# Expert weights in 16 KB pieces per partition, and the order of features that goes with it

## What is computed

```python
mod = c_act @ ada_w[layer] + ada_b[layer]
sh_a, sc_a, g_a, sh_f, sc_f, g_f = jnp.split(mod, 6, axis=-1)
...
h = modulate(rmsnorm(x, norm_ffn[layer]), sh_f, sc_f)
...
g_logits = (h @ w_group) + b_group            # 4 groups
e_logits = (h @ w_expert) + b_expert          # 32 experts
...
(jax.nn.silu(xb @ w_gate[e]) * (xb @ w_up[e])) @ w_down[e]   # 1024 -> 512 -> 1024
...
return jnp.zeros_like(h).at[row_tok].add(ys * row_w[:, None])
```

## Time and profile before

| | before |
|---|---|
| median of 3 runs | 1907.51 us (1904.16 to 1908.43) |
| profiled execution, span | 1901.0 us |
| TensorE busy | 1736.3 us, 91% |
| VectorE busy | 547.8 us, 29% |
| ScalarE busy | 414.4 us, 22% |
| GpSimd busy | 115.6 us, 6% |
| moved by DMA | 548.26 MB in 186871 packets |
| of it on q1 | 492.85 MB in 153536 packets |
| gathers and scatters | 40 and 38 |

### The profile page before, as it was taken

How to read it: one execution, slowest core, us unless ns; L and a number is a source line. 1 busy time by engine, 2 the same in 40 slices (tenths; PEclk the granted TensorE clock), 3 DMA queues, 4 the chain that set the end, 5 groups by cost and what they waited for, 6 DMA issues and landing times.

```text
span 1901.0 us, 17119 instructions
## 1 busy us (share of the span) xinstructions
PE 1736.3 (91%) x6504; PEld 780.1 (41%) x6504; DVE 547.8 (29%) x1218; ACT 414.4 (22%) x1024; POOL 115.6 (6%) x123
## 2 busy tenths in 40 slices
PE   5999998999988889989798999998899988998897
PEld 2455555443433333333344455543433333333332
DVE  2675564431111011101576122225501111111113
ACT  3133354311111011111310234342211111111110
POOL 1000001010000000000000000002000000000000
PEclk9999998999999999999899999999999999999999
DMA  9972423389999999999766021021599999999996
GB/s 347 370 273 84 182 89 136 133 324 380 410 409 410 409 408 406 391 398 395 272 221 221 0 86 48 26 108 59 228 408 410 410 410 408 407 405 405 398 397 256
DMA packets 186871, 548.26 MB, mean 288 GB/s; under 512 B 12345, under 2 KB 49706, under 8 KB 185758
## 3 DMA queue, kind: packets, MB, share of 16 engines
q1 hardware_dynamic: 153536, 492.85, 66.8%
q0 software_dynamic: 15840, 36.64, 5.2%
q10 hardware_dynamic: 17406, 17.59, 2.9%
HBM read 536.66 MB, written 34.63 MB: 301 GB/s over the span
## 4 chain that ended last, share of the span: by engine, by line
PE 65%; DMA 21%; SPq 6%; DVE 5%; issue 2%; ACT 1%; ACTq 0%; DVEq 0%
PE psum L2137 19%; DMA ring<-in_moe_w_up_dram 14%; PE psum L1890 9%; PE psum L1688 9%; PE psum L2170 7%; SPq L447 6%; DMA XN<-in_moe_w_up_dram 4%; PE psum L1743 3%; PE psum L1860 3%; DVE W L1078 1%; DMA XN<-in_moe_w_gate_dram 1%; PE psum L2115 1%; PE psum L1717 1%; PE psum L1617 1%; PE psum L1995 1%
## 5 line engine op out<-in xcount | busy, mean ns | idle before, releaser
L2137 PE MATMUL psum<-ring,V 128*64 128x512 f32 (+1 forms) x1648 | 500.8, 628 | 75.7 <-DMA ring<-in_moe_w_up_dram 49.5
L2137 PEld LDWEIGHTS psum<-ring,V 128*64 128x64 f32 (+1 forms) x1648 | 175.0, 154 | 351.6 <-issue 345.2
L2170 PE MATMUL psum<-ring,V 128*64 128x512 f32 (+1 forms) x832 | 225.1, 597 | 8.2 <-issue 5.1
L973 ACT ACTIVATE V<-psum,modall,scls 128x128 f32<-128x128 f32 x312 | 117.2, 456 | 494.0 <-PE psum L2115 494.0
L1078 DVE SCALAR_TENSOR_TENSOR W<-ring,cact,W 128x512 f32<-128x512 f32 (+1 forms) x224 | 138.5, 618 | 7.7
L1487 DVE TENSOR_TENSOR V<-V,psum 128x512 f32<-128x512 f32 x40 | 27.5, 688 | 378.1 <-PE psum L2137 378.1
L2137 PE MATMUL psum<-XN,V 128*64 128x512 f32 (+1 forms) x288 | 130.7, 607 | 5.4 <-DMA ring<-in_moe_w_up_dram 3.2
L1503 DVE SCALAR_TENSOR_TENSOR HT<-psum,slot_gate,W 128x512 f32<-128x512 f32 x80 | 60.1, 751 | 256.3 <-PE psum L2170 256.3
L2170 PEld LDWEIGHTS psum<-ring,V 128*64 128x64 f32 (+1 forms) x832 | 72.3, 144 | 109.5 <-issue 109.5
L1688 PE MATMUL psum<-HT,ring 128*128 128x512 f32 x256 | 115.4, 597 | 0.0
L982 ACT ACTIVATE V<-psum 128x512 f32<-128x512 f32 x40 | 23.9, 597 | 377.4 <-PE psum L2137 377.4
(11 more groups left out here) (307 smaller groups left out, 1734.2 us busy)
## 6 DMA issues: line engine op xcount, KB each, us to landing
ring<-in_moe_w_gate_dram SPq DMA_DIRECT2D x52, 2048.0 KB, 24.1
ring<-in_moe_w_down_dram SPq DMA_DIRECT2D x52, 2048.0 KB, 24.9
ring<-in_moe_w_up_dram SPq DMA_DIRECT2D x51, 2048.0 KB, 24.9
ring<-in_ada_w_dram SPq DMA_DIRECT2D x16, 2048.0 KB, 15.6
XN<-in_moe_w_gate_dram SPq DMA_DIRECT2D x9, 2048.0 KB, 24.8
XN<-in_moe_w_up_dram SPq DMA_DIRECT2D x9, 2048.0 KB, 26.0
ring<-in_ada_w_dram ACTq DMA_DIRECT2D x16, 1024.0 KB, 5.3
XN<-in_moe_w_down_dram SPq DMA_DIRECT2D x7, 2048.0 KB, 25.8
```

The costliest lines, as they stand in the source:

```text
L973: ins = act.activation(V[:, 2 * D + b * D + k * P:2 * D + b * D + (k + 1) * P], bank[0][:, q * P:(q + 1) * P], ACT.Identity, bias=mod[:, 2 ...
L2137: ins = pe.matmul(bank[2 + 2 * i + b][half * w:(half + 1) * w, :], V[:, col:col + w], slot3(x)[:, k, :], start=(k == 0), stop=(k == KC - 1))
L2170: ins = pe.matmul(bank[6 + hf][half * w:(half + 1) * w, :], V[:, col:col + w], slot3(x, 4)[:, k, hf * HALF:(hf + 1) * HALF], start=(k == 0 ...
```

## The change

The order of features becomes one in which a partition's rows are neighbours in DRAM. For gate and up step k takes feature 8 p + k for partition p, for down it takes 4 p + k. A load is then one contiguous piece of 16 KB for each partition, 128 pieces instead of 512, into the same place. The second norm writes in the new order, reading X with a step of 8 elements; the router weights and the bias columns are loaded in it, by 2 loads instead of 4 and in pieces of 32 bytes instead of 8. A block of 512 modulation features fills only 64 of the 128 partitions in the new order, in 8 columns, so its sum becomes 8 products of 64 columns instead of 4 of 128; a half becomes 8 products of 32 columns instead of 2 of 128. For down, silu and the gate product read PSUM with a step of 4 elements and write V in order. The path for overfull experts, which does not run here, is changed likewise.

```diff
@@ -380,6 +380,14 @@
 
         half_in = [sem(f"half_in{i}") for i in range(2)]
 
+        def ffn_block(i):
+
+            return slice(64 * (i % 2), 64 * (i % 2) + 64), 24 + KC * ((i - 6) // 2), KC * ((i - 6) // 2)
+
+        def ffn_half(i):
+
+            return slice(32 * (i % 4), 32 * (i % 4) + 32), 88 + KC * ((i - 4) // 4), KC * (3 + (i - 4) // 4)
+
         def half_slot(i):
             return ring[:, 5, 2048 * (i % 2):2048 * (i % 2 + 1)].rearrange("p (k n) -> p k n", k=KC)
 
...
@@ -390,14 +398,17 @@
 
             eng.wait_ge(w_in[SLOT[n]], ARRIVED[n])
 
-        def by_pairs(a):
-            return a.rearrange("(a p j) -> p a j", p=P, j=2)
-
         def expert_weights(l, e):
-            g = t["moe_w_gate"][l, ds(e, 1)].rearrange("o (a p j) n -> p (o a) (j n)", p=P, j=2)
-            u = t["moe_w_up"][l, ds(e, 1)].rearrange("o (a p j) n -> p (o a) (j n)", p=P, j=2)
-            d = t["moe_w_down"][l, ds(e, 1)].rearrange("o (k p) n -> p (o k) n", p=P)
+            g = t["moe_w_gate"][l, ds(e, 1)].rearrange("o (p j) n -> p (o j n)", j=KC)
+            u = t["moe_w_up"][l, ds(e, 1)].rearrange("o (p j) n -> p (o j n)", j=KC)
+            d = t["moe_w_down"][l, ds(e, 1)].rearrange("o (p j) n -> p (o j n)", j=4)
             return g, u, d
+
+        def by_fours(a):
+            return a.rearrange("p (q j) -> p j q", j=4)
+
+        def four(a):
+            return a.rearrange("p (j q) -> p j q", j=4)
 
         turned = [sm[1]["pt"], sm[1]["probs"]]
 
...
@@ -517,11 +528,10 @@
                     elif l == 1 and i == 6:
                         sp.wait_ge(*sm[1]["y_added"](2 * TC))
                         sp.wait_ge(*sm[1]["gate_pe"](2))
+                    slot_free(m + i)
+                    sp.dma_start(slot(m + i), {"g": g, "u": u, "d": d}[kind]).then_inc(w_in[SLOT[m + i]], 16)
                     if kind == "d":
-                        load(m + i, d, k=4)
                         del expert[r]
-                    else:
-                        load(m + i, g if kind == "g" else u, k=4)
 
                 rows_back(l)
                 most = sp.value_load(flag[0:1, 0:1], min_val=0, max_val=S)
...
@@ -561,7 +571,7 @@
             for l in range(LAYERS):
                 for i, src in enumerate((t["ada_b"][l, 3 * D:4 * D], t["ada_b"][l, 4 * D:5 * D], t["norm_ffn"][l])):
                     at = (3 * l + i) * KC
-                    pool.dma_start(colF[:, at:at + KC].rearrange("p (a j) -> p a j", j=2), by_pairs(src)).then_inc(col_in, 16)
+                    pool.dma_start(colF[:, at:at + KC], src.rearrange("(p j) -> p j", j=KC)).then_inc(col_in, 16)
             pool.wait_ge(setup_dve, 6)
             pool.dma_start(fb_d, W[0:H, 0:FALL]).then_inc(fb_out, 16)
             pool.wait_ge(fb_out, 16)
...
@@ -592,10 +602,8 @@
                     pool.wait_ge(*s["logits"](N_STEPS))
                 gate_diag(ga_diag[l], mods[l][:, 16:24])
 
-                for j in range(2):
-                    pool.dma_start(rw3[:, j::2, 0:NG], t["moe_w_group"][l].rearrange("(a p j) n -> j p a n", p=P, j=2)[j]).then_inc(s["rw_in"].sem, 16)
-                for j in range(2):
-                    pool.dma_start(rw3[:, j::2, NG:NR], t["moe_w_expert"][l].rearrange("(a p j) n -> j p a n", p=P, j=2)[j]).then_inc(s["rw_in"].sem, 16)
+                pool.dma_start(rw3[:, :, 0:NG], t["moe_w_group"][l].rearrange("(p j) n -> p j n", j=KC)).then_inc(s["rw_in"].sem, 16)
+                pool.dma_start(rw3[:, :, NG:NR], t["moe_w_expert"][l].rearrange("(p j) n -> p j n", j=KC)).then_inc(s["rw_in"].sem, 16)
                 pool.dma_start(rbias[:, 0:NG], t["moe_b_group"][l:l + 1, :].broadcast_to([P, NG])).then_inc(s["rw_in"].sem, 16)
                 pool.dma_start(rbias[:, NG:NR], t["moe_b_expert"][l:l + 1, :].broadcast_to([P, E])).then_inc(s["rw_in"].sem, 16)
 
...
@@ -979,7 +987,7 @@
                     act.wait_ge(*s["gu_pe"](e * 2 + 1))
                     if e >= 2:
                         act.wait_ge(*s["hid_pe"](e - 1))
-                    act.activation(V[:, 4 * D + b * HALF:4 * D + (b + 1) * HALF], bank[2 + b][:, :],
+                    act.activation(four(V[:, 4 * D + b * HALF:4 * D + (b + 1) * HALF]), by_fours(bank[2 + b]),
                                    ACT.Silu).then_inc(s["silu"].sem, 1)
 
                 rows_t(0, 0)
...
@@ -1049,21 +1057,21 @@
-                def normalised(root, ready, c, pairs=False):
+                def normalised(root, ready, c, eights=False):
                     dve.wait_ge(*root(c + 1))
                     step(dve.reciprocal(small[:, 12 + c:13 + c], small[:, 8 + c:9 + c]))
                     to, x = xn3[:, c, :], x3[:, c, :]
-                    if pairs:
-                        to, x = to.rearrange("p (a j q) -> p a j q", j=2, q=P), x.rearrange("p (a q j) -> p a j q", j=2, q=P)
+                    if eights:
+                        to, x = to.rearrange("p (j q) -> p j q", j=KC), x.rearrange("p (q j) -> p j q", j=KC)
                     dve.tensor_scalar(to, x, small[:, 12 + c:13 + c], None, ALU.mult).then_inc(ready.sem, 1)
...
@@ -1082,17 +1090,25 @@
                         ins.then_inc(signal, 1)
 
                 def half_columns(u):
-                    i, n = HALVES_AT[u][0], 2 * len(HALVES_AT[u])
-                    at = 4 * N_MOD0 + 2 * i
                     dve.wait_ge(half_red, u + 1)
-                    bias = colF[:, 3 * KC + 2 * (i - 4):3 * KC + 2 * (i - 4) + n] if 4 <= i < 12 else colA[:, at - 16:at - 16 + n]
-                    dve.tensor_tensor(modall[:, at:at + n], bank[6][:, at:at + n], bias, ALU.add).then_inc(half_col, 1)
+                    for i in HALVES_AT[u]:
+                        at = 4 * N_MOD0 + 2 * i
+                        if 4 <= i < 12:
+                            rows, at, of = ffn_half(i)
+                            ins = dve.tensor_tensor(modall[rows, at:at + KC], bank[6][rows, at:at + KC], colF[rows, of:of + KC], ALU.add)
+                        else:
+                            ins = dve.tensor_tensor(modall[:, at:at + 2], bank[6][:, at:at + 2], colA[:, at - 16:at - 14], ALU.add)
+                    ins.then_inc(half_col, 1)
 
                 def mod_columns(i):
                     dve.wait_ge(mod_red, i + 1)
                     if i == 6:
                         dve.wait_ge(col_in, 16 * 3 * LAYERS)
-                    bias = (colF[:, 4 * (i - 6):4 * (i - 5)] if 6 <= i < 10 else colA[:, 4 * i:4 * i + 4] if i < 12 else
+                    if 6 <= i < 10:
+                        rows, at, of = ffn_block(i)
+                        dve.tensor_tensor(modall[rows, at:at + KC], bank[6][rows, at:at + KC], colF[rows, of:of + KC], ALU.add).then_inc(mod_col, 1)
+                        return
+                    bias = (colA[:, 4 * i:4 * i + 4] if i < 12 else
                             colV[:, V_KAB + 4 * (i - 12):V_KAB + 4 * (i - 11)] if i < 16 else
                             colA[:, 48 + 4 * (i - 16):48 + 4 * (i - 15)])
                     dve.tensor_tensor(modall[:, 4 * i:4 * i + 4], bank[6][:, 4 * i:4 * i + 4], bias, ALU.add).then_inc(mod_col, 1)
...
@@ -1310,7 +1326,7 @@
                     dve.wait_ge(*s["y_added"](u + 1))
                     for ch in norms_at.get(u, ()):
                         mean_square(s["ss2"], s["arg2"], ch)
-                        normalised(s["root2"], s["xn2"], ch, pairs=True)
+                        normalised(s["root2"], s["xn2"], ch, eights=True)
 
                 for k in (2, 3, 6, 7):
                     dve.wait_ge(*s["xt2_pe"](KC // 2 + k // 2 + 1))
...
@@ -1483,8 +1499,8 @@
                 def hidden(e, b):
                     dve.wait_ge(*s["silu"](e + 1))
                     dve.wait_ge(*s["gu_pe"](e * 2 + 2))
-                    at = V[:, 4 * D + b * HALF:4 * D + (b + 1) * HALF]
-                    dve.tensor_tensor(at, at, bank[4 + b][:, :], ALU.mult).then_inc(s["hid"].sem, 1)
+                    at = four(V[:, 4 * D + b * HALF:4 * D + (b + 1) * HALF])
+                    dve.tensor_tensor(at, at, by_fours(bank[4 + b]), ALU.mult).then_inc(s["hid"].sem, 1)
 
                 def hidden_t(e, b):
                     dve.wait_ge(*s["hid_pe"](e + 1))
...
@@ -1612,10 +1628,14 @@
                 else:
                     pe.wait_ge(mod_sum, i - 3)
                 pe.wait_ge(mod_col, i)
-                for j in range(4):
-                    by_two = slice(2 * P * (j // 2) + j % 2, 2 * P * (j // 2 + 1), 2)
-                    ins = pe.matmul(bank[6][:, 4 * i + j:4 * i + j + 1], acc[:, by_two if 6 <= i < 10 else slice(j * P, (j + 1) * P)],
-                                    C[:, C_32:C_32 + 1] if i < 4 else ones[:, 0:1], start=True, stop=True)
+                if 6 <= i < 10:
+                    rows, at, _ = ffn_block(i)
+                    for j in range(KC):
+                        ins = pe.matmul(bank[6][rows, at + j:at + j + 1], acc[:, j::KC], ones[:, 0:1], start=True, stop=True)
+                else:
+                    for j in range(4):
```

(42 more changed lines are left out.)

## The result

The changed kernel takes 1997.94 us (median of 4 runs, 1989.37 to 2008.28) beside 1907.97 us for the kernel before on the same chip (1904.16 to 1908.65): a ratio of 1.049, 95% interval 1.047 to 1.052. It is slower by 90 us, where the forecast said slower by 22 us. The direction was right, the size was not, and the time lies outside the range.

A forecast was written before the change was run, and what follows sets the result against it. Weight transfers were taken to bound the expert stages, with longer pieces making gathers late. Stages +17.5 us and small parts +5 gave 22.5 on 1901.0, 1923.5; with 6.5 to the runs' median, 1930 us, range 1868 to 1955.

The forecast's parts named there:

- Rate: Expert weight loads: 16 KB pieces move at 429 GB/s instead of 410, worth 22 us a layer, 44 in all.
- Turns by packet: DMA engines alternate between weight and row queues packet by packet; a turn grows from 0.27 to 0.69 us, scatter-gather pair 12.4 us.
- The loop: Expert stage: down, scatter, gather, transposes, down form a cycle of 26.5 us a pass, taken as 26.2.
- 7.9 for transposes and down products: Last part of the expert pass cycle: TensorE's transposes of gathered rows and down products, put at 7.9 us.
- worse turns: Rival: two weight packets pass per row packet, turn 1.30 us, expert pass 37.5 us, total over 2300 us; chance 0.13.
- The small parts: Side costs outside the weight loads: modulation columns, halves, norm, PSUM reads and initial column loads, together +5 us (-2 to +16).
- (1): Layer 0 modulation columns, four blocks: eight 64-wide products replace four 128-wide, +0.4 us each, +1.6 on TensorE's path.
- Term (2): Layer 1, eight modulation halves: eight 32-wide products replace two, 0.63 to about 1.0 us each, +2.4 us (0 to 7.2).
- Term (3): Second norm reading X with a step of 8: +0.7 us each (0 to 1.5), +1.4 us in the sum.
- Term (4): Silu and gate product reading PSUM with step 4: open only in each layer's last pass, taken as +0.2 us.
- The gather stays hidden: Rival: expert-stage gathers still hide, leaving only the rate gain, 1868.5 us, or half hidden 1885 to 1903; chance 0.22.
- Pieces cut again: Rival: 16 KB weight pieces are cut into 4 KB packets, leaving only the small parts, 1912.5 us; chance 0.15.

The follow-up runs named there:

- early gathers: Each gather issued one pass sooner, ahead of the scatter it stood behind: on the changed kernel 1884.69 us (ratio 0.990), on the kernel before 1903.3 us (0.999).
- the version by fours: Changed kernel with early gathers, features 512 a + 4 p + j, gate and up in 8 KB pieces, four modulation products: 1883.65 us; with gathers not moved 1887.55 us.

## Why the prediction was right, and where it failed

- *Rate.* Right in kind: 426 GB/s at 16 KB and 420 at 8 KB where 429 and 423 came from the line. Its worth was put at 22 us a layer; where nothing covers it, with early gathers on both sides, the stages fall by 518.9 - 505.2 = 13.7 and 519.3 - 502.3 = 17.0. Most of the rest is in the first pass of each layer, which takes 4.5 and 3.8 us longer, counted from its gather's issue; over the 19 passes behind it the gain is 18.2 (470.6 against 452.4) and 20.8 (469.8 against 449.0). These 452.4 us are 23.8 a pass, so the pace of the weights was put 1 us too high, at 24.8.
- *Turns by packet.* Right. While a scatter and a gather go out beside weights, the two queues of the changed kernel (514 to 524 us: packets, MB, share) take turns one for one, whatever the size of either's packets:

```profile
q1 hardware_dynamic: 264, 3.80, 88.8%
q0 software_dynamic: 263, 0.48, 12.5%
```

  That is 10 x 16 / 264 = 0.61 us a turn in the mean, against 0.69 forecast. The 3.80 MB are 232 pieces of 16 KB; the other 32 of the 264 are small packets, which come with each load, 16 to one (the version with 4 KB pieces, which makes two loads of each of the 192, has 192 x 16 = 3072 packets more on q1 than the kernel before: 156608). In a stretch without rows, 528 to 538 us, they stand alone under 512 B:

```profile
DMA packets 293, 4.28 MB, mean 428 GB/s; under 512 B 32, under 2 KB 32, under 8 KB 32
```

  A full piece took 0.888 x 160 / 232 = 0.61 us and a row 0.125 x 160 / 263 = 0.08. So a turn with a full piece is the forecast's 0.69; what the forecast lacked is that every eighth turn goes against a small packet. The pair of scatter and gather takes 18 x 0.61 = 10.9 us by that, not 12.4. The landings fit. Behind a scatter a gather lands in 8.0, 10.2 and 15.1 us at 4, 8 and 16 KB, 0.59 us for each KB (16 turns of 37 ns); without a scatter ahead of it (early gathers) in 7.4, 8.4 and 10.7, 0.28 for each KB (7 to 8 turns).
- *The loop.* Right, 26.2 us forecast. Measured 28.0 in layer 0 and 27.7 in layer 1 with slow down products; the four passes of the trace in which both halves ran at the full clock took 25.3 (539.54 to 564.87) to 25.9 (456.70 to 482.62), less than forecast, as the shorter turns would have it.
- *The step that failed* is "7.9 for transposes and down products". Its cause, a pause of 3 to 4 us ahead of them in each pass, was written further on, as a thing that the profile would show; that the clock might fall in it was not asked. The first half of down took 4.5 to 6.0 us in 14 of the 15 passes that the chain lists behind 482.62 us in layer 0, 5.2 in the mean instead of 3.5, and the transposes ahead of it up to 1.11 instead of 0.66: some 2 us a pass, about 65 us in 34. Against the forecast the two stages miss 39.4 - 7.1 and 38.5 - 10.4, 60 us together, and the slow products cover them. That the pause is their cause is shown by the run in which products on constants fill it: 52 us of the time went away. None of the rivals had it; "worse turns" gave a like time for another reason.
- *First gather.* +4 forecast, +2.7 measured in layer 0 (10.04 against 7.37); in layer 1 it took 9.95 us.
- *The small parts* were forecast as +5 (-2 to +16). The six kernels that share the order by eights have 402.8 to 405.8 us to the first gather (394.8 and 397.8 in the two kernels with the old one) and 450.8 to 459.7 between the stages (447.5 and 450.0): +8.7 and +7.8 in the mean, 16 us (the two old ones, alike up to the first gather, differ by 3.0 there). The mis-sized term is (1): a modulation block takes 2.08 us on the timeline instead of 1.05, +1.0 and not +0.4, and the same with four 128-wide products in steps of 4 (the version by fours):

```profile
90.80 2.08 PE L1634 MATMUL psum<-C,W 128*64 128x1 f32 x16
...
92.81 8.83 PE L1708 MATMUL psum<-ring,HT 128*128 128x512 f32 x16
```
```profile
90.42 1.97 PE L1629 MATMUL psum<-C,W 128*128 128x1 f32 x8
```

  The first two rows are of the 16 KB version with early gathers, the third of that by fours. The products behind the eight short ones took 8.83 us where the same 16 take 7.1 in the others: in each of the six kernels with the 2.08 us blocks this happened at least once, in none of the four with the old order or with fours. In the changed kernel the window at that place has PEclk 0.51 between two at 1.00:

```profile
84.00:89.00 5.00, 5.00 (x13) 2.09 (x11) 4.79 (x7) 0.00 (x0) 0.00 (x0) 1.00 0.85 316
91.60:94.60 3.00, 3.00 (x4) 1.01 (x4) 2.83 (x5) 0.00 (x0) 0.00 (x0) 0.51 1.04 406
```

  So 4 x 1.0 and one to two times 1.7 make up most of the 8.7. That the short products bring the lower clock is read from where it falls and is not shown, since no run changed them alone. Term (2), the halves: 1.15 us for one and 1.91 for two, where 0.52 to 0.63 and 0.99 to 1.10 stood in the old order; the eight together take 8.4 us instead of 4.4, +4.0, where +2.4 was forecast. Term (3), the norm: 1.15 us instead of 0.75, +0.4 and not +0.7. Term (4), step 4 on reads from PSUM: silu 597 ns and product 688 ns in both kernels, nothing, where 0.2 a layer had been set. Of the 7.8 between the layers these terms leave some 3 us open.
- *Rivals.* "The gather stays hidden" would have been the right picture with 8 KB pieces or early gathers; its point of decision, a turn of 0.60, was close to the 0.61 measured. Yet between them lies not a small step but the fall of the clock: where TensorE waits 3 to 4 us in a pass, another 2 come on top in most. "Pieces cut again" was forecast at 1912.5; the kernel made so takes 1915.5.

## What to carry to other kernels

Longer pieces raise the rate of a stream (410 to 426 GB/s here) and lengthen the turn that every small packet of another queue waits for (0.27 to 0.61 us); so look for gathers with little slack beside it, and move their issue ahead before the pieces grow, or stop at the size that leaves them hidden. When a forecast puts a new wait of some microseconds ahead of TensorE's work in each pass, price the products behind it at the lower clock too. The best version here takes gathers issued a pass earlier and pieces of 8 and 16 KB; it is 1.1% faster than the kernel before (1.0% with 16 KB pieces throughout and early gathers, which is level with it), where the long pieces alone are 4.9% slower.

## What was not expected of the hardware

- In the changed kernel the products behind a wait of 4.11 us ran at 0.50 for some 3 us; those behind waits of 2.73 (554.05) and 2.89 us (471.81) kept their 3.65 us a half. The length of the wait alone does not decide it: behind waits of 2.87 (1518.07) and 2.85 us (1879.71) the first half took 5.1 and 5.3 us, and behind one of 3.17 (1714.71) it took 3.65. What does decide it stays open.
- The 128-wide weights of a column product, read with a step of 4 elements, take twice the time of those with a step of 1 or 2: 0.25 us a record on the timeline (1.97 / 8) against 0.13 (1.05 / 8). With a step of 8 a record of 64 columns takes 0.13 (2.08 / 16), for each column again twice the old time. VectorE's norm behaves alike: 0.75 us with steps 1 and 2, 1.15 with step 8, 1.16 with step 4. Reads of PSUM with a step of 4 cost nothing on ScalarE (597 ns) or VectorE (688 ns). The Trainium skill (SBUF — State Buffer, the note on cachelines under Door 1) has full rate while two accesses fall into 16 bytes; for float32 that puts the border between steps 2 and 4, where these rows have it. The same note names 4 float32 as a free stride; VectorE's 1.16 us at a step of 4 goes against that.
